# A large pair's product with V between scores and turns; low half of the output from the turn bank; three turn banks and one output bank

## The reference

```python
scores = jnp.einsum('bnqrhd,bnkrhd->bnrhqk', qb, kk,
                    preferred_element_type=jnp.float32) * (dh ** -0.5)
scores = jnp.where(valid[None, :, None, None], scores, NEG_INF)
lse = jax.nn.logsumexp(scores, axis=-1)
p = jnp.exp(scores - lse[..., None])
o = jnp.einsum('bnrhqk,bnkrhd->bnqrhd', p.astype(v.dtype), vv)
...
w = jax.nn.softmax(jnp.stack(lses, axis=0), axis=0)
o = jnp.einsum('gbsh,gbshd->bshd', w, jnp.stack(outs, axis=0).astype(jnp.float32))
...
mix = jnp.concatenate([attn, u], axis=-1)
x = x + mix @ w_out[layer].astype(mix.dtype)
```

## Time and profile before

| | |
|---|---|
| median of 3 timed runs | 2442.02 us (2441.14 to 2442.36) |
| the profiled execution's own time | 2445.07 us |
| its span in the profile | 2443.2 us |
| PE busy | 98% of the span |
| DVE, ACT, POOL busy | 63%, 33%, 6% |
| attention, layer 0 | about 252 to 409 us |
| attention, layer 1 | about 1466 to 1619 us |

### The profile page before, as it was taken

One profiled execution on the slowest core, in us unless ns is written; L12 is line 12 of the kernel. 1 busy time (PEld: TensorE's weight loads), 2 busy tenths in 40 slices (PEclk: granted clock), 3 DMA queues, 4 the chain that ended last, 5 costly groups with the idle time before them and its releaser, 6 DMA issues.

```text
span 2443.2 us, 30713 instructions
## 1 busy us (share of the span) xinstructions
PE 2392.1 (98%) x11672; PEld 1948.9 (80%) x11672; DVE 1548.8 (63%) x1659; ACT 801.5 (33%) x1066; POOL 156.9 (6%) x57
## 2 busy tenths in 40 slices
PE   7999999999999999999999998999999999999999
PEld 6888777888888888888878887778888888888887
DVE  5999764656555555555649997646655555555555
ACT  4222665432222222222332227744322222222221
POOL 0122001100000000000012120011000000000000
PEclk9999999999999999999999999999999999999999
DMA  4324541111111111111112244301211111111111
GB/s 154 91 78 116 131 90 27 43 52 52 52 52 52 43 52 43 51 44 50 43 31 82 78 138 113 79 18 44 67 46 51 35 52 52 52 43 52 44 51 69
DMA packets 46676, 153.44 MB, mean 63 GB/s; under 512 B 7424, under 2 KB 10112, under 8 KB 46592
## 3 DMA queue, kind: packets, MB, share of 16 engines
q1 hardware_dynamic: 45728, 149.93, 21.1%
q10 hardware_dynamic: 864, 2.36, 0.2%
HBM read 131.02 MB, written 21.23 MB: 62 GB/s over the span
## 4 chain that ended last, share of the span: by engine, by line
PE 89%; issue 5%; DVE 3%; ACT 2%; POOLq 0%; DMA 0%; DVEq 0%; POOL 0%; SPq 0%; ACTq 0%
PE mm L477 59%; PE aux L477 20%; PE aux L632 3%; PE aux L613 3%; PE mm L589 2%; PE aux L504 1%; DVE sc L1306 1%; DVE y L1176 1%; ACT sc L909 0%; PE aux L513 0%; DMA x<-xT 0%; POOLq L1485 0%; DVE x_lo L1102 0%; PE aux L570 0%; DVE w_lo L1090 0%
## 5 line engine op out<-in xcount | busy, mean ns | idle before, releaser
L477 PE MATMUL mm<-x_hi,w_hi 128*128 128x512 f32 x1952 | 609.8, 394 | 17.8 <-DVE x_lo L1102 11.8
L477 PE MATMUL mm<-x_hi,w_lo 128*128 128x512 f32 x1952 | 604.9, 391 | 0.0
L477 PE MATMUL mm<-x_lo,w_hi 128*128 128x512 f32 x1952 | 604.5, 391 | 0.0
L477 PEld LDWEIGHTS mm<-x_hi,w_hi 128*128 128x128 f32 x1952 | 364.2, 188 | 97.4 <-issue 12.0
L477 PEld LDWEIGHTS mm<-x_lo,w_hi 128*128 128x128 f32 x1952 | 367.2, 188 | 79.7
L477 PEld LDWEIGHTS mm<-x_hi,w_lo 128*128 128x128 f32 x1952 | 367.0, 188 | 79.1
L776 ACT ACTIVATE w_hi<-w_raw 128x1024 fp32r<-128x1024 f32 x154 | 162.0, 1059 | 659.5 <-PE mm L477 461.2
L1096 DVE TENSOR_TENSOR x<-x,aux 128x1024 f32<-128x1024 f32 x176 | 214.8, 1220 | 121.3 <-PE aux L477 111.6
L1090 DVE TENSOR_TENSOR w_lo<-w_raw,w_hi 128x1024 fp32r<-128x1024 f32 x154 | 196.6, 1282 | 55.2 <-ACT w_hi L776 51.2
L1108 DVE TENSOR_TENSOR uv<-mm,rinv 128x1024 f32<-128x1024 f32 x44 | 53.9, 1225 | 220.0 <-PE mm L477 219.8
L1176 DVE SCALAR_TENSOR_TENSOR y<-u_all,cpar,y 128x512 f32<-128x512 f32 x248 | 186.5, 765 | 0.1
(11 more groups left out here) (191 smaller groups left out, 2987.9 us busy)
## 6 DMA issues: line engine op xcount, KB each, us to landing
w_raw<-weights SPq DMA_DIRECT2D x188, 512.0 KB, 3.6
qk_scratch<-m SPq DMA_DIRECT2D x64, 128.0 KB, 2.1
qk_scratch<-o SPq DMA_DIRECT2D x64, 128.0 KB, 2.1
x_hi<-qk_scratch SPq DMA_DIRECT2D x32, 256.0 KB, 6.4
q_first<-qk_scratch SPq DMA_DIRECT2D x8, 512.0 KB, 4.8
k_hh_first<-qk_scratch SPq DMA_DIRECT2D x16, 256.0 KB, 6.0
k_ll_first<-qk_scratch SPq DMA_DIRECT2D x16, 256.0 KB, 6.5
x_hi<-qk_scratch SPq DMA_DIRECT2D x8, 512.0 KB, 4.6
```

The costliest lines, as they stand in the source:

```text
L477: last = pe.matmul(acc[:, cols], a, b[:, cols], start=start and n == 0, stop=stop and n == 2)
```

## The change

It does four things. A third turn bank: the fills go round three banks, the two of `stat_b` and the first of `stat_s`; the second of `stat_s` is the only output bank, so that pair 0 of every head waits until the head before has been moved out. The pairs: pair 3 moves from step 6 to step 7 of its head and pair 2 from step 10 to step 11 (step 3 of the next head), and these two stand between the scores and the turns of their step and no longer behind the turns. The low part: DVE takes it from the turn bank itself, as soon as ACT has written the high part; ACT's copy L927 is gone, and it is DVE that frees the bank. Behind the loop the product with ones waits for all three turn banks, and the first piece of the output projection goes from step 67 to step 68 of the loop, which keeps it behind the last head's pair 2.

```diff
-ATTENDS = ((5, 0), (6, 3), (9, 1), (10, 2))
+ATTENDS = ((5, 0, 2), (7, 3, 3), (9, 1, 6), (11, 2, 7))
...
-assert PT % 2 == 0
+TURN_BANKS = 3
+BANK_FILLS = [len(range(b, PT, TURN_BANKS)) for b in range(TURN_BANKS)]
...
+        turn_bank = [stat_b[:, 0:BANK], stat_b[:, BANK:], stat_s[:, 0:BANK]]
+        o_bank = stat_s[:, BANK:]
...
+        def bank_read(l, f, after=0):
+
+            return at(l, BANK_FILLS[f % TURN_BANKS], f // TURN_BANKS + 1 + after)
...
-                    bank = stat_b[:, f % 2 * BANK:(f % 2 + 1) * BANK]
-                    pe.wait_ge(pt_read[f % 2], at(l, PT // 2, f // 2 + 1))
+                    bank = turn_bank[f % TURN_BANKS]
+                    pe.wait_ge(pt_read[f % TURN_BANKS], bank_read(l, f))
+                    if f == 2:
+
+                        pe.wait_ge(v_turned, at(l, PAIRS, PAIRS))
...
-                    at_step, pair = ATTENDS[k]
+                    _, pair, second = ATTENDS[k]
                     b, hh = h // 2, h % 2
                     if h == 0 and k == 0:
                         pe.wait_ge(v_turned, at(l, PAIRS, PAIRS))
-                    if k == 0 and (l or h >= 2):
-
-                        pe.wait_ge(o_moved, at(l, HEADS, h - 1))
-                    for bank in range(2):
-                        fills = [f for f in range(LAST_FILL[h * TB + at_step - 3] + 1) if f % 2 == bank]
-                        pe.wait_ge(pt_read[bank], at(l, PT // 2, len(fills) + 1))
-                    cols = slice(hh * BANK + pair * P, hh * BANK + (pair + 1) * P)
+                    if k == 0 and (l or h):
+
+                        pe.wait_ge(o_moved, at(l, HEADS, h))
+                    last_fill = LAST_FILL[h * TB + second]
+                    for f in range(max(0, last_fill + 1 - TURN_BANKS), last_fill + 1):
+                        pe.wait_ge(pt_read[f % TURN_BANKS], bank_read(l, f, 1))
+                    cols = slice(pair * P, (pair + 1) * P)
                     for kb in range(2 * pair + 2):
                         for half in range(2):
                             if kb <= 2 * pair + half:
-                                last = pe.matmul(stat_s[half * HEAD_DIM:(half + 1) * HEAD_DIM, cols],
+                                last = pe.matmul(o_bank[half * HEAD_DIM:(half + 1) * HEAD_DIM, cols],
...
-                    if n == STEPS + 3:
+                    if n == STEPS + 4:
...
+                    attends = [((n - first) // TB, k) for k, (first, _, _) in enumerate(ATTENDS)
+                               if (n - first) % TB == 0 and 0 <= n - first < STEPS]
+                    for h, k in attends:
+                        if k % 2:
+                            attend(h, k)
                     for f in range(PT):
                         if FILLS[f][0] == n and FILLS[f][1] == "p":
                             turn(f)
-                    for k, (at_step, _) in enumerate(ATTENDS):
-                        if (n - at_step) % TB == 0 and 0 <= n - at_step < STEPS:
-                            attend((n - at_step) // TB, k)
+                    for h, k in attends:
+                        if k % 2 == 0:
+                            attend(h, k)
...
+                for bank in range(TURN_BANKS):
+
+                    pe.wait_ge(pt_read[bank], at(l, BANK_FILLS[bank], BANK_FILLS[bank] + 1))
                 for half in range(2):
                     cols = slice(half * BANK, (half + 1) * BANK)
-
-                    pe.wait_ge(pt_read[half], at(l, PT // 2, PT // 2 + 1))
                     last = pe.matmul(stat_b[:, cols], ones[:], y_sum[:, cols], start=True, stop=True)
...
-                            "p (k q) -> p k q", q=P), ACT.Copy).then_inc(pt_read[f % 2], 1)
+                            "p (k q) -> p k q", q=P), ACT.Copy).then_inc(pt_read[f % TURN_BANKS], 1)
                     else:
                         act.activation(x_hi[:, which, a * BANK:(a + 1) * BANK], bank, ACT.Copy).then_inc(o_hi, 1)
-                        act.activation(o_nat[:, a * 4:(a + 1) * 4, :], bank.rearrange("p (b c) -> p b c", c=P),
-                                       ACT.Copy).then_inc(pt_read[f % 2], 1)
...
-                    act.activation(o_turned[h % 2], stat_s[:, h % 2 * BANK:(h % 2 + 1) * BANK], ACT.Copy
+                    act.activation(o_turned[h % 2], o_bank, ACT.Copy
...
-                    fills = [g for g in range(f + 1) if g % 2 == f % 2]
-                    dve.wait_ge(pt_read[f % 2], at(l, PT // 2, len(fills) + 1))
+                    dve.wait_ge(o_hi, at(l, 2 * PAIRS, 2 * which + a + 1))
                     out = (slice(None), which, slice(a * BANK, (a + 1) * BANK))
-                    dve.tensor_tensor(x_lo[out], rinv[:, a * BANK:(a + 1) * BANK], x_hi[out].bitcast(F32),
-                                      ALU.subtract)
-                    dve.drain().then_inc(o_split, 1)
+                    dve.tensor_tensor(x_lo[out], turn_bank[f % TURN_BANKS], x_hi[out].bitcast(F32),
+                                      ALU.subtract).then_inc(o_split, 1)
+                    dve.drain().then_inc(pt_read[f % TURN_BANKS], 1)
 
```

9 lines of the change are left out of this document (5 added, 4 removed).

## The result

| | before | after |
|---|---|---|
| timed runs beside each other, median (lowest to highest) | 2442.19 us (2441.14 to 2443.16, 4 runs) | 2427.03 us (2426.80 to 2429.83, 4 runs) |
| the profiled execution's own time, and its span | 2445.07, 2443.2 us | 2427.01, 2425.2 us |
| ratio, with its 95% interval | | 0.9942 (0.9926 to 0.9957) |

The change makes the kernel 15 us faster, 0.58%.

What follows compares the result with a forecast made beforehand. PE, busy 98%, could gain only from its waits, ended by DVE and ACT chains. Per layer -1.2 (quiet heads) - 4.7 (full heads) + 0.3 (end) = -5.6; two layers -11.2, from 2442.02 to 2430.8 us, range 2422 to 2438.

Steps and rivals of the forecast that it cites:

- the chain of the full heads: In heads with two "o" fills, DVE and ACT alternate (mask, exp, read, copy, low part) while PE waits; still limiting at 17.7 us.
- the quiet heads' price: Heads without "o" fills: the third bank removes PE's 0.34 us wait for a turn bank; 1.2 us per layer.
- The floor: PE's busy time per head, 15.95 us without "o" fills, 17.11 with two; nearest floor, 17 us of gain, 2425 us.
- Full head: Head with two "o" fills: 0.39 (pair 3), 0.98 (low part), 0.20 (pair 2), 1.57 us together, three times per layer.
- off the path: In heads without "o" fills, removing exp 7's 0.39 us wait for its mask was claimed to gain nothing.
- First full head: The layer's first head with two "o" fills, counted like the other two at 1.57 us gained.
- That a bank is held until DVE is done costs nothing.: Turn bank of an "o" fill: holding it longer was priced at nothing, its next fill coming three fills later.
- DVE reading PSUM: Low part read from the turn bank: priced at nothing; the skill's rule would cost an estimated 65 ns each.
- The end: Behind the last head: exp of step 7 0.39 us earlier, product with ones +0.7 for the low parts; net +0.3 per layer.
- The clock: Rival, 0.09: two low-clock stretches in layer 0, 3.4 us together, may vanish with shorter waits; 2427.5 us.
- The slower rival: Rival, 0.07: pair 2 lands on the path to exp 3, 1.5 us in each of 14 heads; 2451 us.
- The slack: In heads with two "o" fills, 0.3 us between the end of ACT's reads of step 1's turns and of mask 3.

Runs made afterwards that it cites:

- e3: The changed kernel with ACT's copy into SBUF kept and the low part taken from that copy: 2432.89 us, ratio 0.9962.
- e1: The changed kernel with pairs 3 and 2 back in their old places behind the turns: 2437.32 us, ratio 0.9977.
- e11: The kernel before with three turn banks and one output bank alone, the product with ones waiting for all three: 2448.68 us, ratio 1.0023.
- e2: The kernel before with only pairs 3 and 2 moved, two turn banks and ACT's copy kept: 2432.33 us, ratio 0.9960.
- e6: The changed kernel with ACT's exp of step 7 ahead of its reads of step 5's turns: 2421.85 us, ratio 0.9920.
- e7: The changed kernel with DVE's mask of the next step ahead of the low part: 2420.16 us, ratio 0.9913.
- e4: The kernel before with only the low part taken from the turn bank and ACT's copy gone: 2439.42 us, ratio 0.9989.
- e5: The kernel before with pairs moved and low part from the turn bank, two turn banks and two output banks: 2430.13 us, ratio 0.9950.

## Why the prediction was right, and where it was not

The time lay in the range, and the chain of the full heads was the one forecast. One step was wrong, the quiet heads' price, at about half of what they gave; that the time lay in the range all the same is owed to the range's width and not to that step.

*Where the time came from.* Per layer the eight cuts span 7.06 us less, and the end is 0.30 longer. The forecast's terms were 1.2 + 4.7 and +0.3. The rest of the 18.0 between the two spans is the clock (8.60 - 7.06 = 1.54 between the cuts and 1.68 at the end of layer 0, 20.87 against 19.19 us at full clock) and 1.22 ahead of the attention, where the change touches nothing. So the order of the work gave 13.5 us over two layers where 11.2 were forecast, and the timed medians differ by 15.2. The floor that the prediction took from PE's busy time, 15.95 us for a quiet head, was none: the head takes 15.79 now, with 15.07 of them busy.

*Full head: 1.57 forecast, 1.75 measured.* Right, in size and by its chain: masks 1 and 3 within 0.2 us of where they were put. The terms are another matter. With three banks, removing the copy gives 0.94 (e3; 0.98 forecast) and moving the pairs 0.50 (e1: 17.98 to 17.48; 0.39 + 0.20 forecast). The third bank, priced at nothing there, gives 0.31 alone (e11). So two terms were a little high and one was missing; that the sum is as near as it is is partly luck.

*Quiet head: 0.34 forecast, 0.71 measured. This step failed.* It said that the third bank takes the 0.34 wait away and that the earlier exp 7 "is off the path" here. The bank alone gives 0 (e11, 16.50 as before; the low part beside it, e1, adds nothing), the pairs alone 0.48 (e2), the bank on top of them 0.23. With both in place exp 7 is still on the path: putting it ahead of the reads gives a further 0.33 (e6). The mask and exp 7, held by the late read-out, lay beside the bank wait and were a little longer. The trace of before had the row that says so: ACT's 0.39 for the mask of step 7. I followed the bank wait's own chain, and didn't ask whether PE, with that wait gone, would be waiting for the mask that was late too. In layer 1 the four quiet periods gave 0.48 (the first) and 0.68 to 0.73, together 2.61 where 1.2 was forecast; the three full ones gave 4.45 where 4.7 was.

*First full head: 0.95 measured, 1.57 forecast.* This stretch (19.67 before, 18.72 after) has POOL's sum in it and a tap on DVE that takes 2.75 us, where the others take 0.75. It is the forecast's second wrong term, and the table says which part is missing: moving the pairs gives 0.50 here as in the other full heads (e1: 19.22), but removing the copy 0.45 and not 0.94 (e3: 19.17), and the third bank nothing (e11: 19.68, at a clock of 0.98). e7, which takes the low parts out of the masks' way, brings it to 17.15. That the long tap is the reason was not tested.

*"That a bank is held until DVE is done costs nothing."* Right for the change, by the third bank and not by itself: with two it costs PE a wait of 0.98 (e4) or 0.76 (e5). This is what the third bank is for. The parts taken alone give 10.1 (e2), 3.0 (e4) and -5.8 us (e11), 7.3 together; the whole gives 15.2. By the estimate above much of that gap is e11's clock. In heads at full clock the parts alone give a full head 0.80 + 0.19 + 0.31 = 1.30, the whole 1.75, and a quiet one 0.48, the whole 0.71.

*DVE reading PSUM: nothing.* Right: 0.69 us before and after. The rule of the Trainium skill that the prediction weighed (VectorE: DVE Perf Modes, on the TRN2 errata), an estimated 65 ns more for each, isn't seen for this shape.

*The end: +0.3 forecast, +0.30 measured,* of a wait of 0.51 that is new, less the earlier last exp. The size is right, the reason only in part: the prediction gave the +0.7 to the low parts that must be out of the banks. With the low parts from the banks and each half waiting for its own (e5) the product begins at 16.82 behind the last cut, no later than with the pairs alone and the copy kept (e2, 16.81); with the copy kept and the wait for all three banks (e3) it is 17.38. It is the wait for all three banks ahead of the first half that costs.

*The clock.* A rival with 9%, told as 3.4 us. It was no rival but an addition: 3.2 us of the profile's difference are its two stretches. Of the timed medians only the 15.2 - 13.5 = 1.7 us left over can be its share, and nothing shows that they are. What the records of the single runs do show is that the falls come and go between executions of one kernel: of the 21 runs of the kernel before beside e1 to e4 the five longest (2444.3 to 2445.5 us) have a mean clock of 0.998, the others 0.999 or 1.000, and of the change's four the one at 2429.83 us has 0.999, the other three 1.000.

*The slower rival.* Pair 2 never came on the path: mask 1 was where it had to be, and the reads of step 1's turns (375.24 for 0.98) end at 376.22, while exp 3 waits until 376.52 for its mask. The slack is 0.30, as the forecast had it.

## What to carry to other kernels

Where two waits of one length have different releasers and stand within a microsecond of each other, take neither's length as its worth: move one in thought and see what the engine does at the other. A buffer that is handed from a fast reader to a slow one may need one more of its kind, and each of the two edits can look nearly useless or harmful if tried by itself, as here. An edit that lets an instruction wait for more buffers than it writes has a price of its own (here 0.77 us a layer). And when all waits earlier in a period are gone but the chain that sets it is not, the idle time gathers into one piece in front of it: look at the granted clock behind that piece before calling an edit neutral.
